# Router products on unscaled tokens, scores scaled per token, batched steps of expert choice, and low parts made on GpSimd

## The reference

```python
h = h + jnp.concatenate([oa, ob], axis=-1) @ w_out[i]
h = h + hier_moe(rms_norm_2(h, g_ffn[i]), w_rg[i], w_re[i], w1[i], w3[i], w2[i])
...
def hier_moe(x, w_rg, w_re, w1, w3, w2):
    g_prob = jax.nn.softmax((xf @ w_rg).astype(jnp.float32), axis=-1)
    g_gate, g_idx = lax.top_k(g_prob, 1)
    e_logits = (xf @ w_re).astype(jnp.float32).reshape(t, N_GROUPS, EXPERTS_PER_GROUP)
    e_logits = jnp.take_along_axis(e_logits, g_idx[:, :, None], axis=1)[:, 0]
    e_w, e_i = lax.top_k(jax.nn.softmax(e_logits, axis=-1), TOP_K)
    weights = g_gate * (e_w / jnp.sum(e_w, axis=-1, keepdims=True))
    experts = (g_idx * EXPERTS_PER_GROUP + e_i).astype(jnp.int32)
    ...
    hdn = jax.nn.silu(xb @ w1[e]) * (xb @ w3[e])
    return hdn @ w2[e]
```

## Time and profile before

| | |
|---|---|
| timed runs | 1608.0, 1609.68, 1610.2 us; median 1609.68 |
| span of the profiled execution | 1607.5 us |
| TensorE / VectorE / ScalarE / GpSimd busy | 97% / 45% / 33% / 10% |
| DMA, mean | 194 GB/s |
| out-projection's last product | ends at about 1035 us |
| first product of the gather | at about 1059 us |

### The profile page before, as it was taken

How to read it: one execution, slowest core, us unless ns; L and a number is a source line. 1 busy time by engine, 2 the same in 40 slices (tenths; PEclk the granted TensorE clock), 3 DMA queues, 4 the chain that set the end, 5 groups by cost and what they waited for, 6 DMA issues and landing times.

```text
span 1607.5 us, 19630 instructions
## 1 busy us (share of the span) xinstructions
PE 1556.4 (97%) x7802; PEld 1090.3 (68%) x7802; DVE 718.2 (45%) x1208; ACT 531.7 (33%) x910; POOL 162.9 (10%) x172
## 2 busy tenths in 40 slices
PE   6999999999999999999999999999999999999898
PEld 5776688789888888887877777754444444444366
DVE  5334332445444445458756787543132132132164
ACT  5333332335423334235355577331111011010042
POOL 1012200101211102020400210011000000000000
PEclk9999999999999999999999999999999999999999
DMA  7111142222222222232101132689999999999961
GB/s 269 37 69 60 62 161 105 92 80 92 105 82 102 105 105 105 83 114 80 53 27 53 66 122 76 266 308 359 420 422 421 421 421 419 420 421 421 422 246 54
DMA packets 45437, 311.22 MB, mean 194 GB/s; under 512 B 5136, under 2 KB 5648, under 8 KB 10016
## 3 DMA queue, kind: packets, MB, share of 16 engines
q1 hardware_dynamic: 42336, 296.22, 46.2%
q0 software_dynamic: 3008, 13.72, 2.4%
HBM read 301.52 MB, written 8.39 MB: 193 GB/s over the span
## 4 chain that ended last, share of the span: by engine, by line
PE 88%; DVE 4%; DMA 3%; ACT 3%; issue 2%; DVEq 0%; ACTq 0%; POOLq 0%
PE bank L788 21%; PE bank L2457 13%; PE bank L831 8%; PE bank L1382 6%; PE bank L2473 6%; PE bank L840 5%; PE bank L2440 4%; PE bank L2490 4%; PE bank L1242 3%; PE bank L2656 3%; DMA M<-in_w 3%; PE bank L857 1%; PE bank L1024 1%; PE bank L1069 1%; PE bank L800 1%
## 5 line engine op out<-in xcount | busy, mean ns | idle before, releaser
L612 DVE TENSOR_TENSOR w_lo<-M,w_hi 128x2048 fp32r<-128x2048 f32 x73 | 168.8, 2318 | 184.9 <-ACT w_hi L607 184.9
L2457 PE MATMUL bank<-M 128*64 128x512 f32 x1024 | 227.4, 595 | 3.8 <-DMA M<-in_w 3.8
L607 ACT ACTIVATE w_hi<-M 128x2048 fp32r<-128x2048 f32 x73 | 139.0, 1911 | 158.3 <-PE bank L788 56.9
L788 PE MATMUL bank<-HTH,w_hi 128*128 128x512 f32 x432 | 168.1, 389 | 0.0
L788 PE MATMUL bank<-HTL,w_hi 128*128 128x512 f32 x432 | 168.1, 389 | 0.0
L788 PE MATMUL bank<-HTH,w_lo 128*128 128x512 f32 x432 | 168.0, 389 | 0.0
L2457 PEld LDWEIGHTS bank<-M 128*64 128x64 f32 x1024 | 71.5, 137 | 139.3 <-issue 138.2
L2473 PE MATMUL bank<-M 128*64 128x512 f32 x512 | 114.0, 595 | 2.0 <-DMA M<-in_w 1.9
L2615 DVE TENSOR_TENSOR X<-bank,X 128x512 f32<-128x512 f32 x69 | 46.6, 689 | 112.6 <-PE bank L2490 112.5
L788 PEld LDWEIGHTS bank<-HTL,w_hi 128*128 128x128 f32 x432 | 81.1, 188 | 16.9
L788 PEld LDWEIGHTS bank<-HTH,w_lo 128*128 128x128 f32 x432 | 81.1, 188 | 16.9
(11 more groups left out here) (365 smaller groups left out, 2907.4 us busy)
## 6 DMA issues: line engine op xcount, KB each, us to landing
M<-in_w SPq DMA_DIRECT2D x192, 1024.0 KB, 10.1
M<-in_wd SPq DMA_DIRECT2D x78, 1024.0 KB, 4.9
M<-in_nb SPq DMA_DIRECT2D x4, 1536.0 KB, 6.4
X<-in_x SPq DMA_DIRECT2D x4, 512.0 KB, 9.4
M<-in_rows POOLq DMA_DIRECT2D x4, 512.0 KB, 6.0
M<-in_tb POOLq DMA_DIRECT2D x8, 256.0 KB, 4.4
rowb<-in_rows POOLq DMA_DIRECT2D x4, 512.0 KB, 5.9
xs_parts<-XSH POOLq DMA_DIRECT2D x1, 2048.0 KB, 11.1
```

What stands on the lines that cost most here:

```text
L607: e.activation(hi[:, :], slots[slot_of[n]], ACT.Copy).then_inc(split_hi_done, 1)
L612: e.tensor_tensor(lo[:, :], slots[slot_of[n]], hi[:, :], ALU.subtract).then_inc(split_lo_done, 1)
L788: m = e.matmul(out[:, :], w[:, k0 + k, n0:n0 + 128], v[k], start=(k == 0 and i == 0), stop=(k == len(hi) - 1 and i == 2))
L2457: m = e.matmul(b[64 * s:64 * s + 64, :], Xe[:, 4 * kh + k, o + C * s:o + C * s + C], unit_w(key, 4)[:, k, :], start=(kh == 0 and k == 0), ...
```

## The change

Ahead of everything, VectorE multiplies the router weights with the gain of the norm, once (288 elements a partition, in the stage of differential attention, after the weights have landed). In `out2`, TensorE transposes X itself, not the scaled tile. The transposes need only the additions to X. In the router's products the operands change places: XNT's 128 tokens are the array's weights, the 36 columns of the router weights move, so that tokens stand in rows. VectorE multiplies the result with r while it reads the bank (`score_dve`) and writes it to L. The way back (a ScalarE copy, a transpose, a copy) is gone. Transposes and router products are written earlier in TensorE's list, between the halves of the out-projection. The lists of ScalarE and VectorE are reordered to go with it: a "score" step stands where a "keep" stood, tile 3's additions stand behind the score of tile 1, and ScalarE's high parts of tiles 2 and 3 stand last. The low parts are made by GpSimd (`keep_pool`), ahead of its DMA issues.

In the choice, the groups of four operations become single ones over all tiles. PRE is gone: TensorE sums SEL itself, with three products of ones that add to the ranks and four for the totals. Ranks are counted from 1 (`iota` starts at 1), so that the subtraction of one is gone. The total's maximum is read later (`rounds_dve`). The one-hot matrix is signalled tile by tile, and the gather waits tile by tile. One bank less is claimed, which moves the turn of the banks behind it by one.

```diff
         def norm_pe(e, R, t):
-            if R != 4:
+            if R < 3:
                 e.wait_ge(n_scaled, 4 * R + t + 1)
...
+                if R == 3:
+                    taken(e, ("o2", t, h))
                 b, fills = claim(e, ("n", R, t, h))
+                src = X[:, t, :] if R == 3 else norm_xs(R, t)
...
+            e.wait_ge(d_wr, 16)
+            e.tensor_tensor(wr[:, :, :], wr[:, :, :], col("g_route", 0, 8).unsqueeze(2).to_broadcast([128, KD, 36]),
+                            ALU.mult).then_inc(wr_done, 1)
...
-                if t == 2:
-                    norm_pe(e, 3, 0)
-            norm_pe(e, 3, 1)
+                    if (t, h) == (2, 0):
+                        norm_pe(e, 3, 0)
+                    if (t, h) == (3, 0):
+                        norm_pe(e, 3, 1)
+                        route_logits_pe(e, 0)
             norm_pe(e, 3, 2)
-            for t in range(2):
-                route_logits_pe(e, t)
+            route_logits_pe(e, 1)
             norm_pe(e, 3, 3)
...
-            for t, s in ((0, 0), (1, 0), (0, 3), (0, "keep"), (2, 0), (1, 3), (1, "keep"), (3, 0), (2, 3), (2, "keep"), (3, 3),
+            for t, s in ((0, 0), (0, 3), (0, "keep"), (1, 0), (1, 3), (2, 0), (1, "keep"), (2, 3), (3, 0), (3, 3), (2, "keep"),
                          (3, "keep")):
...
-            for h in range(2):
-                filled(e, ("n", 3, 3, h))
+            for t in range(TT):
+                keep_pool(e, t)
             e.wait_ge(n_keep_lo, TT)
...
-                m = e.matmul(b[0:36, 0:128], wr[:, k, :], XNT[:, k, t * 128:(t + 1) * 128], start=(k == 0), stop=(k == KD - 1))
+                if k % 4 == 0:
+                    taken(e, ("n", 3, t, k // 4))
+                m = e.matmul(b[:, 0:36], XNT[:, k, t * 128:(t + 1) * 128], wr[:, k, :], start=(k == 0), stop=(k == KD - 1))
             m.then_inc(fills, 1)
...
-            e.wait_ge(rt_pre, 1)
-            e.matmul(b[:, 32:128], con("ones"), flat(PRE[:, 0:3, :]), start=False, stop=True)
-            e.matmul(b[:, 128:160], con("ones"), PRE[:, 3, :], start=True, stop=True).then_inc(fills, 1)
+            for t in range(1, TT):
+                e.matmul(b[:, 32 * t:128], con("ones"), flat(SEL[:, 0:TT - t, :]), start=False, stop=(t == TT - 1))
+            for t in range(TT):
+                m = e.matmul(b[:, 128:160], con("ones"), SEL[:, t, :], start=(t == 0), stop=(t == TT - 1))
+            m.then_inc(fills, 1)
...
+        def score_dve(e, t):
+            b, empties = filled(e, ("rl", t))
+            e.tensor_scalar(L[:, t, :], b[:, 0:36], NORM_ST[3][t][2], None, ALU.mult).then_inc(empties, 1)
...
-            for t in range(TT):
-                c = e.tensor_tensor(by_group(prod, t), L[:, t, 4:36].rearrange("p (g e) -> p g e", g=4),
-                                    goh[:, t, :].unsqueeze(2).to_broadcast([128, 4, 8]), ALU.mult)
-            dve_own.mark(c)
+            dve_own.mark(e.tensor_tensor(by_group(prod), by_group(L[:, :, 4:36]), goh.unsqueeze(3).to_broadcast([128, 4, 4, 8]),
+                                         ALU.mult))
```

More of the change, by code:

```diff
@@ L404, in build @@
             ps.put(("rl", t), [next(ROUTE_AT)])
[L406 removed]
+        for key in (("pl", 0, 0), ("pl", 0, 1), ("pl", 1, 0), "rk", ("pl", 1, 1), ("pl", 2, 0)):
             ps.put(key, [next(ROUTE_AT)])
@@ L2167, in out2_dve @@
                     taken(e, ("o2a", t, h))
[L2168 to L2171, removed]
+            for t, s in ((0, 0), (0, 1), (1, 0), (0, 3), (1, 1), (0, "score"), (2, 0), (1, 3), (2, 1), (1, "score"), (3, 0), (2, 3),
+                         (3, 1), (3, 3), (2, "score"), (3, "score")):
+                if s == "score":
+                    score_dve(e, t)
                     continue
@@ L2276, in route_act @@
         def route_act(e):
-            for t in range(TT):
-                b, empties = filled(e, ("rl", t))
-                e.activation(LT[0:36, t * 128:(t + 1) * 128], b[0:36, 0:128], ACT.Copy).then_inc(empties, 1)
             for at in ((0, 0), (0, 1), (1, 0)):
@@ L2319, in route_dve @@
             e.wait_ge(dve_own.sem, dve_own.n)
-            for t in range(TT):
-                c = e.tensor_tensor(by_group(SEL, t), s8[:, t, :].unsqueeze(1).to_broadcast([128, 4, 8]),
-                                    goh[:, t, :].unsqueeze(2).to_broadcast([128, 4, 8]), ALU.mult)
-            c.then_inc(rt_sel, 1)
-            e.wait_ge(rt_sel, 1)
-            dve_own.mark(e.tensor_copy(PRE[:, 0, :], SEL[:, 0, :]))
-            for t in range(1, TT):
-                e.wait_ge(dve_own.sem, dve_own.n)
-                c = e.tensor_tensor(PRE[:, t, :], PRE[:, t - 1, :], SEL[:, t, :], ALU.add)
-                if t < 3:
-                    dve_own.mark(c)
-            c.then_inc(rt_pre, 1)
+            e.tensor_tensor(by_group(SEL), s8.unsqueeze(2).to_broadcast([128, 4, 4, 8]), goh.unsqueeze(3).to_broadcast([128, 4, 4, 8]),
+                            ALU.mult).then_inc(rt_sel, 1)
             e.tensor_tensor(ge_, GL, per_token(gm, 4), ALU.subtract).then_inc(rt_wexp_in, 1)
@@ L2374, in weights_dve @@
             e.wait_ge(dve_own.sem, dve_own.n)
-            for t in range(TT):
-                c = e.tensor_tensor(by_group(W32, t), w8[:, t, :].unsqueeze(1).to_broadcast([128, 4, 8]),
-                                    goh[:, t, :].unsqueeze(2).to_broadcast([128, 4, 8]), ALU.mult)
-            c.then_inc(rt_w32, 1)
+            e.tensor_tensor(by_group(W32), w8.unsqueeze(2).to_broadcast([128, 4, 4, 8]), goh.unsqueeze(3).to_broadcast([128, 4, 4, 8]),
+                            ALU.mult).then_inc(rt_w32, 1)
         XET = [area(22528 + 2048 * i, 8, 256) for i in range(2)]
@@ L3146, in _layout @@
         "b_gate", "pool_scale", "conv_w", "conv_b",
-        "g_sub_2")] + [_tiles(np.tile(i[n].reshape(-1), 4)) for n in ("g_qb_2", "g_kb_2")], axis=1)
+        "g_sub_2")] + [_tiles(np.tile(i[n].reshape(-1), 4)) for n in ("g_qb_2", "g_kb_2")]
+                          + [_tiles(i["g_ffn_2"].reshape(-1))], axis=1)
     rows = np.concatenate([i[n].reshape(-1) for n in (
```

65 lines of the change are left out of this document (28 added, 37 removed).

## The result

The changed kernel takes 1610.37 us (median of 20 runs, 1608.1 to 1614.1), the one before 1609.04 us in the 20 runs beside it. The ratio is 1.0013, 95% interval 1.0007 to 1.0019: 2.1 us more, between 1.1 and 3.1, and less than the 0.2% that the prediction takes for no change. Predicted were 1610.6 us and 1606.5 to 1613.8.

What follows compares the result with a forecast made beforehand. A chain through four engines before the first gather was taken as the bound. Without turns the gather came 2.1 us earlier; turns of 3.1 us made it 0.9 later, added to the median 1609.68: 1610.6 us, range 1606.5 to 1613.8.

Steps and rivals of the forecast that it cites:

- The place: From the last out-projection products to the first gather, a stretch of 24 us hangs on a chain through four engines.
- the transfer to the end: Behind the first gather: a shift of its start was carried to the kernel's end one to one, in either direction.
- The late addition: VectorE's additions to tile 3 wait for tile 1's logits and score; the last tile's sum comes 2.2 us late.
- first step of choice: Start of the choice on VectorE: forecast at 1046.8 against 1048.69 before, a gain of 1.9 us.
- turns and a slow clock: Rival: beside the turns, TensorE idles from 1051.8 to 1054.8 and its clock falls; +2.5 us in all, 1612.2; chance 0.22.
- The turns: In the choice, GpSimd's subtractions for tiles 2 and 3 block two-input VectorE operations by whole instructions: two waits, 3.1 us.
- No turns and no fall: Rival: the choice's small operations slip between GpSimd's subtractions; gather 2.1 us earlier, 1607.6; chance 0.18.
- the four cases within 3.2 us: Turns without the clock 0.40, turns with the clock 0.22, no turns 0.18, weight stream hides it all 0.06; called same, 0.85.
- Selection steps: VectorE's steps from the start of the choice to the end of the selection: 4.66 us left of 5.35.
- Rank products: TensorE's eight products for the ranks in place of three: 1.76 us, a loss of 0.2 to 0.35 us.
- Subtractions on GpSimd: The low parts, four 128x1024 subtractions moved from VectorE to GpSimd: 2.6 us each.
- Batched steps alone: In the choice, three groups of four small operations become one operation each: 0.7 us saved.

Runs made afterwards that it cites:

- e6: e2 with the low parts of tiles 2 and 3 made by VectorE after the selection is handed over; 1608.15 us, ratio 0.9997.
- e1: The changed kernel with all four low parts made by VectorE again, at their places in the kernel before; 1612.22 us, ratio 1.0029.
- e3: The changed kernel with each router product moving 144 columns, of which 36 are read; 1613.64 us, ratio 1.003.
- e2: The changed kernel with VectorE's additions to tile 3 put ahead of the score of tile 1; 1608.81 us, ratio 0.9999.
- e9: The changed kernel with the low parts of tiles 2 and 3 made by VectorE after the selection, 36 columns kept; 1611.40 us, ratio 1.0019.
- e5: The changed kernel with the edits of e2 and e3 together; 1610.26 us, ratio 1.0009.
- e10: The changed kernel with the low parts of tiles 2 and 3 late on VectorE and router products moving 144 columns; 1607.36 us, ratio 0.9991.
- e4: The kernel before with only the steps of the choice batched over the four tiles; 1607.82 us, ratio 0.9996.
- e7: e6 with VectorE copying tile 3's second transposed half ahead of scaling tile 3; 1605.67 us, ratio 0.9982.
- e11: A second profile of the changed kernel, with nothing altered; 1609.93 us in a single execution.

## Why the prediction was right, and where it was not

**The place: right; the transfer to the end: right to 1.6 us.** The stretch between the out-projection and the gather decides, and its shift reaches the end: in ten of eleven kernels the shift by the runs is within 1.6 us of the one in the profile; e6, at 1.8, is the exception. Inside the changed kernel's profile the shift is still +2.45 at 1477, and 1.2 us of it come back in the last pairs, where TensorE waits for weights (7.96 of 10 us busy from 1500 on, as before). From 1490 to 1500 it is busy for 10.00 us, for 9.62 before: that is slack of the stream, used up. One to one, as the prediction has it, is not what this profile shows. The losses of e1 and e3 came through whole (4.9 and 4.7, 4.5 and 4.8).

**The late addition: right.** The prediction had the last eight products of tile 1 at 1040.58 and the additions over at 1042.0; measured are 1040.25 and 1041.73, the same to 0.1 us with the start taken off. It called this order the thing that takes back most of the gain, and e2, which turns one entry round, gives 3.0 us back in the stretch and 2.3 by the runs, though with a turn in it and a fall that comes later and is shorter in its profile.

**The step that failed: the clock ahead of the choice.** The prediction has the first step of choice at 1046.8 and used as its evidence a stop of TensorE in which the clock held. That row is from a kernel whose next products moved 128 columns. The change itself makes them 36 wide, and in those products the clock fell to 0.50 in both profiles of the changed kernel, in e1 and in e9. The sum priced them at 0.22 us each; the sixteen of tiles 2 and 3 took 6.68 us, 0.42 each. The first step of choice came at 1050.13 in place of 1046.8. The rival "turns and a slow clock" was nearer in its size (+2.5 against +2.6) but put the fall behind 1052, as an addition to the turns; of the profiles only e3's has that one.

**The turns: right as a mechanism, wrong in size and place.** Forecast were two waits with 3.1 us together; there is one, of 1.8 to 2.0 us (e2, e3, e5). The first step is a reduction with one input and isn't held up, and the choice begins at the end of tile 2's subtraction or up to 0.2 us behind it, not ahead of it. In the changed kernel the wait isn't there at all. An unforeseen one is, off the path: tile 1's scaling took 1.90 us in place of 1.28 beside GpSimd. In the rows that the term was read from, GpSimd's subtraction ends at 404.01, 1.14 us behind VectorE's end at 402.87, not 1.2 to 1.3, and VectorE's ends 0.15 us ahead of the place given for it; that changes nothing in the sum.

**So the forecast of 1610.6 was right by a wrong sum:** -1.9 at the first step, -0.7 for the steps, +3.1 for the turns and +0.35 for the ranks were to give +0.9; what happened was +1.8 -0.6 +1.4 and no turns, +2.6. That the number lay near was luck. The turns were added to a choice that starts early, and the early fall moves the choice out of their reach: those two exclude each other. (Of the chances, the four cases within 3.2 us add up to 0.86, not 0.85.)

**No turns and no fall: too good by about 0.8 us.** The forecast was -2.1. e10 has -0.66 with wide products, which cost about 0.25 us for each of two tiles (1.98 for 1.72 us) and 0.16 us on the last four products (1.26 against e2's 1.10): some -1.3 with narrow ones, an estimate. The missing part is small: two scores of 0.26 with 0.24 us idle behind the last, where 0.2 stood once.

**The rest.** Selection steps 4.75 us for 4.66 forecast. Rank products 1.71 for 1.76. Subtractions on GpSimd 2.35 to 2.77 for 2.6. Batched steps alone 0.6 (e4) for 0.7. The scaling of the router weights and the later row and copies on GpSimd's queue show in no chain piece of this stretch; they weren't tried by themselves.

**What stays open.** What sets off the fall. It came in six of the seven profiles of e1, e2, e6, e7, e9 and the changed kernel (twice) whose router products move 36 columns, behind stops of 0.4 to 2.2 us and in e7 without any, and in none of the six with 128 or 144 columns at this place, with stops up to 1.6 us. A stop isn't needed for it, then, by e7; what else decides isn't shown, and each of these kernels but the changed one has a single profile. It lasted 3.4 us in e2 and e7 and about 10 in the others, which had stops of 1.0 us and more. Of the changed kernel's 20 timed runs one has a trace, and e11 is a second. For the others there is the granted clock as a mean over the execution: 0.991 to 0.995 with the median 0.993, against 0.994 to 0.999 with the median 0.995 in 80 runs of the kernel before. A fall of 10 us to one half is worth 0.003 of that mean, so most of the 20 fit with the long fall. The six at 0.995 are among the quickest (1608.1 to 1609.8 us); in them it may be shorter or missing, which isn't shown. e2's profile is of its quickest execution, with a mean of 0.997; seven of its eleven have 0.993 to 0.995 and took 1606.7 to 1610.5 us, so longer falls than the 3.4 us of the trace are likely in them.

## What to carry to other kernels

Before a cost is read off a stop that did no harm, ask what the engine does behind it in the new kernel: a stop that was harmless ahead of one kind of product may not be ahead of another. Where two costs compete for the same moment, don't add them; ask which comes first and whether it moves the other out of reach, and test them as a square, since removing either alone may show nothing. The remedy was cheap and in the order, not in the arithmetic: what TensorE waits for next goes first on VectorE (the addition, then the copy), and long GpSimd subtractions are kept away from a chain of short VectorE steps with two inputs.

## What the runs showed of the hardware

- TensorE's granted clock fell to 0.50, the 1.2 GHz level, for 10 us behind a stop of 1.0 us (changed kernel, both profiles, and e9), while TensorE was busy in every microsecond of the fall from 1042 on; sixteen router products took 6.68 us in place of 3.60 at the full level (e7). With 144 columns moved by each product the same stop was followed by no fall (e3, e10).
- A 144-column router product costs 0.25 us and a 36-column one 0.22 us, eight of them 1.98 and 1.72 us: a quarter of the width saves an eighth of the time.
- One 128x1024 subtraction on GpSimd with two inputs takes 2.35 us, on VectorE 1.22 to 1.23. It holds a VectorE operation with two inputs that starts behind it until it ends (2.13 us for 0.17 in e2), and not a reduction (0.17).
- GpSimd is held too: its subtraction beside tile 2's scaling took 2.77 us in place of 2.35 to 2.39 (changed kernel).
- Four operations of 32 elements each in one of 128 take 0.29 us in place of 0.50.
